# First seven rotary tiles on VectorE with their splits in turn, and sums, chunk roundings and second root moved in the passage between attention and feed-forward

## What is computed

```python
h = modulate(rms_norm(x, g_pre_mix), sh1, sc1)
qa, ka, va, qi, ki, wi, qb, kb, vb, ga, gb = project(h, pos, w_in)   # rope on qa, ka, qi, ki, qb, kb
oa, ob = mixer(qa, ka, va, qi, ki, wi, qb, kb, vb)                   # top-k attention, differential attention
m = sigmoid(ga) * (oa @ w_o_a) + sigmoid(gb) * (ob @ w_o_b)
x = x + gt1 * rms_norm(m @ w_out, g_post_mix)
h = modulate(rms_norm(x, g_pre_ffn), sh2, sc2)
f = (silu(h @ w_gate) * (h @ w_up)) @ w_down
x = x + gt2 * rms_norm(f, g_post_ffn)
```

## Time and profile before

| | us |
|---|---|
| median of 3 runs | 1034.13 |
| the profiled execution, its own time | 1035.23 |
| its span, first to last instruction | 1033.4 |
| PE busy in it | 964.7 (93%) |
| DVE, ACT, POOL busy | 443.1, 410.7, 375.5 |

### The profile page before, as it was taken

How to read it: one execution, slowest core, us unless ns; L and a number is a source line. 1 busy time by engine, 2 the same in 40 slices (tenths; PEclk the granted TensorE clock), 3 DMA queues, 4 the chain that set the end, 5 groups by cost and what they waited for, 6 DMA issues and landing times.

```text
span 1033.4 us, 17731 instructions
## 1 busy us (share of the span) xinstructions
PE 964.7 (93%) x7100; PEld 916.0 (89%) x7100; DVE 443.1 (43%) x869; ACT 410.7 (40%) x766; POOL 375.5 (36%) x181
## 2 busy tenths in 40 slices
PE   4887997999998999999999779999999999999995
PEld 1686897999998989988888679999999999999995
DVE  5786637898885233332100834333333333000005
ACT  4754334556556555443333733222222222222221
POOL 2131025556262331234554124444443343444440
PEclk9898998999999999999999889999999999999998
DMA  9821012222221113357855012222222221322212
GB/s 368 316 75 46 7 63 87 102 102 85 90 99 51 41 49 131 111 221 256 304 191 187 22 41 82 82 82 81 81 81 81 81 81 56 105 73 82 82 54 92
DMA packets 35600, 111.61 MB, mean 108 GB/s; under 512 B 4240, under 2 KB 9360, under 8 KB 35280
## 3 DMA queue, kind: packets, MB, share of 16 engines
q1 hardware_dynamic: 31152, 102.48, 29.0%
q10 hardware_dynamic: 4112, 6.93, 1.8%
q0 software_dynamic: 272, 1.31, 0.3%
HBM read 100.38 MB, written 10.32 MB: 107 GB/s over the span
## 4 chain that ended last, share of the span: by engine, by line
PE 75%; issue 9%; DVE 7%; ACT 4%; DMA 3%; POOL 2%; ACTq 0%; DVEq 0%; SPq 0%; POOLq 0%
PE pj L1831 25%; PE pj L1598 23%; PE pj L1870 12%; PE pvb L1728 3%; DMA raw<-in_w_ada 3%; PE pj L1607 2%; PE lg L1570 2%; PE tb L1712 2%; PE pj L1843 1%; DVE kz L1277 1%; PE lg L1893 1%; PE lg L1895 1%; PE lg L1894 1%; DVE ro L552 1%; DVE mb L1340 1%
## 5 line engine op out<-in xcount | busy, mean ns | idle before, releaser
L1076 POOL TENSOR_TENSOR wlo<-raw,whi 128x1024 fp32r<-128x1024 f32 x53 | 131.1, 2474 | 202.8 <-ACT whi L724 196.9
L1132 POOL TENSOR_TENSOR wlo<-raw,whi 128x1024 fp32r<-128x1024 f32 x41 | 105.2, 2567 | 183.7 <-ACT whi L1043 183.7
L1831 PE MATMUL pj<-hh,wlo 128*128 128x288 f32 (+1 forms) x640 | 137.4, 296 | 0.0
L1831 PE MATMUL pj<-hh,whi 128*128 128x288 f32 (+1 forms) x640 | 137.1, 295 | 0.0
L1831 PE MATMUL pj<-hl,whi 128*128 128x288 f32 (+1 forms) x640 | 136.9, 295 | 0.0
L1598 PE MATMUL pj<-hh,whi 128*128 128x288 f32 x544 | 124.7, 311 | 4.9 <-ACT zs L805 4.0
L1598 PE MATMUL pj<-hh,wlo 128*128 128x288 f32 x544 | 117.9, 298 | 0.0
L1598 PE MATMUL pj<-hl,whi 128*128 128x288 f32 x544 | 117.9, 299 | 0.0
L1831 PEld LDWEIGHTS pj<-hh,wlo 128*128 128x128 f32 x640 | 103.4, 189 | 0.0
L1831 PEld LDWEIGHTS pj<-hh,whi 128*128 128x128 f32 x640 | 102.9, 188 | 0.0
L1831 PEld LDWEIGHTS pj<-hl,whi 128*128 128x128 f32 x640 | 102.8, 188 | 0.0
(11 more groups left out here) (216 smaller groups left out, 2015.0 us busy)
## 6 DMA issues: line engine op xcount, KB each, us to landing
raw<-in_w_s SPq DMA_DIRECT2D x94, 512.0 KB, 3.5
rawa<-in_w_ada SPq DMA_DIRECT2D x32, 512.0 KB, 6.1
rawd<-in_w_d SPq DMA_DIRECT2D x16, 704.0 KB, 4.1
raw<-in_w_ada SPq DMA_DIRECT2D x16, 512.0 KB, 10.1
g_raw<-gz ACTq DMA_DIRECT2D x16, 288.0 KB, 2.1
gate<-g_raw SPq DMA_DIRECT2D x8, 576.0 KB, 3.9
rawv<-in_w_v SPq DMA_DIRECT2D x8, 324.0 KB, 5.0
xt<-in_xT SPq DMA_DIRECT2D x2, 1152.0 KB, 6.7
```

What stands on the lines that cost most here:

```text
L1076: pool.tensor_tensor(wlo[:, slot(c), :], raw_of(c), whi[:, slot(c), :].bitcast(F32), ALU.subtract)\
L1132: pool.tensor_tensor(wlo[:, slot(c), :], raw[:, raw_slot(c), :], whi[:, slot(c), :].bitcast(F32), ALU.subtract).then_inc(w_lo, 1)
L1831: ins = mm(pj[tile % 2][:, h, 0:HALF + 2 * h], w[:, slot(C_GU + q), b:b + P], x[h][:, kc, :], start=(kc == 0 and w is whi and x is hh2), s ...
```

## The change

`N_VEC` is 7: kb0 and qb0 are turned on DVE as well. For these seven the split stands right behind the tile's `end` (and the rounding of value chunks), and `hi` behind the split; the split of qb0 so stands ahead of the three top-k rounds. kb1 keeps POOL, and its split stays in unit 2. In the passage POOL sums the squares of tiles 0 to 5 only and `stat1` takes a third matmul for tile 6; `hi(C_GU+2)` and the second root move behind `scaled(1, 4)`, `hi(C_GU+3)` and `hi(C_GU+4)` ahead of the last root, and `ada_ends(5)` behind the first half's work on DVE. `N_SUM0` renumbers the counts of POOL's sums.

```diff
+N_VEC = ROPE_AT[("qb", 0)] + 1
 def schedule():
-    def project(c, waiting, values=()):
-
-        s.extend([("part", AT[c], 0, KC)] * (AT[c] >= N_FIRST) + [("split", w) for w in waiting] + [("end", AT[c])]
-                 + [("vsplit", k) for k in values])
-        return [AT[c]]
-
-    last = []
+    def project(c, values=()):
+
+        s.extend([("part", AT[c], 0, KC)] * (AT[c] >= N_FIRST) + [("end", AT[c])] + [("vsplit", k) for k in values])
+        if ROPE_AT[c] < N_VEC:
+            s.extend([("split", AT[c]), ("hi", AT[c])])
+
     for c, values in zip(ROPES[:N_KI], ((4, 5), (6, 7), (), (), ())):
-        last = project(c, last, values)
-    s += [("split", c) for c in last] + [("vload",)]
+        project(c, values)
+    s += [("vload",)]
...
-    last = project(("kb", 0), [])
-    last = project(("qb", 0), last)
+    project(("kb", 0))
+    project(("qb", 0))
     topk(3)
-    last = project(("kb", 1), last)
+    project(("kb", 1))
...
-    split_in[2] = last
+    split_in[2] = [AT[("kb", 1)]]
...
+        N_SUM0 = (KC - 1) + (KC - 2)
...
             act.activation(hf1[1][:, :, HALF:HALF + 2], ada[:, 3 * KC:4 * KC, :], ACT.Copy).then_inc(shift_ready, 1)
-            hi(C_OUT + KC - 1 + RING)
...
                 scaled(1, kc)
-                if kc == 1:
+                if kc == 4:
                     act.wait_ge(rstd_ready, 2)
                     act.wait_ge(stat_full, 3)
                     rms_half(0)
+                    hi(C_GU + 2)
                 if kc % 2:
                     squares_x1(1, kc // 2)
+            hi(C_GU + 3)
+            hi(C_GU + 4)
             act.wait_ge(rstd_ready, 3)
...
-                        if c < C_DN:
+                        if 0 < t and c < C_DN:
...
-                        if r >= N_KI:
+                        if r >= N_VEC:
                             turns_of(pool, c, r)
...
-                if d < KC - 1:
+                if d < KC - 2:
                     squares(0, d, acc1, sq1)
...
-                    if ROPE_AT.get(CH[s[1]], N_KI) < N_KI:
+                    if ROPE_AT.get(CH[s[1]], N_VEC) < N_VEC:
                         rope(s[1])
...
-            for n in range(3, 6):
+            for n in range(3, 5):
                 ada_ends(n)
...
             for h in range(2):
+                if h:
+                    ada_ends(5)
                 v.wait_ge(ysq_ready, KC + h)
...
             def stat1(h):
-                stat_half(h, [acc1, sq1[:, KC - 1, :]], [(acc_ready, 2 * (KC - 1)), (ysq_ready, KC + h)])
+                stat_half(h, [acc1, sq1[:, KC - 2, :], sq1[:, KC - 1, :]],
+                          [(acc_ready, N_SUM0), (ysq_ready, KC - 1), (ysq_ready, KC + h)])
```

More of the change, by code:

```diff
@@ L1109, in squares @@
                 if d:
-                    pool.wait_ge(acc_ready, (n + 1) * (KC - 1) + d)
+                    pool.wait_ge(acc_ready, (N_SUM0 if n else KC - 1) + d)
                 pool.tensor_tensor(acc[:, :], acc[:, :], sq[:, d, :], ALU.add).then_inc(acc_ready, 1)
             def y_tile(d):
-                if d < KC - 1:
+                if d < KC - 2:
                     squares(0, d, acc1, sq1)
@@ L1847, in stat3 @@
             def stat3(h):
-                for i, (x, sem_, n) in enumerate(((acc2[:, :], acc_ready, 3 * (KC - 1)),
+                for i, (x, sem_, n) in enumerate(((acc2[:, :], acc_ready, N_SUM0 + KC - 1),
                                                   (sq2[:, KC - 1, :], ysq_ready, 2 * KC + 1 + h))):
```

## The result

| | kernel before | changed kernel |
|---|---|---|
| median (lowest to highest), us | 1033.71 (1033.14 to 1037.04), 4 runs | 1017.58 (1015.15 to 1019.73), 4 runs |
| profiled execution, us | 1035.23 | 1019.73 |
| its span, us | 1033.4 | 1017.6 |

The ratio is 0.9833, 95% interval 0.9814 to 0.9852: faster by 16.1 us, where 20.0 were predicted. The time lies in the range of 1009 to 1022, 3.6 above the number given. The page of the changed kernel, first part (compare): PE has four matmuls more, the third product of `stat1`, and loses less around its work.

The account below looks back on a forecast made before the run. PE, busy 93% of the span, was taken to lose most of its time up to the feed-forward in four waits (5.37, 5.38, 5.65, 4.51 us). Terms 6.0, 4.0 and 10.0 sum to 20.0; 1034.1 less 20.0 is 1014, range 1009 to 1022.

Parts of the forecast that it names:

- The passage, 10.0: Passage into the feed-forward: reordered sums, roots and roundings remove PE's waits, gaining 10.0 us; ends 7.0 and 10.5.
- (e): Passage: hi(C_GU+3), hi(C_GU+4) run beside stat2(1); the 4.51 wait goes, following tiles at full clock end near 612.5, not 623.
- The clock rival: Head and passage: remaining waits bring 1.2 GHz back each time; head 5.0, passage 7.5, time 1017.6; chance 0.14.
- the prediction's last sign of being wrong: Behind the short waits: a granted clock near 0.66 would show the prediction wrong.
- The head, 6.0: First five rotary tiles: hi behind the split frees ro, first indexer head 6.0 us earlier; ends 3.1 and 7.1.
- clock term, +0.5: Head: +0.5 us, taken between up to 1.6 more from the indexer's clock and up to 0.8 less from the last lo.
- the tile count: Head: a tile falls from 7.05 to 6.55 us; counted through, the last rest comes 5.5 earlier.
- kb0 and qb0, 4.0: Ahead of attention unit 0: six DVE instructions of 0.75 replace six POOL ones of 1.42, gaining 4.0; ends 2.5 and 7.0.
- The race: kb0: DVE's second rest instruction, issued at 153.45, narrowly passes POOL's lo at 153.6; losing costs 1.5 us.
- The rival of the shared way: Head and kb0: POOL's shifted subtraction falls fully on the next tile's products; neither wins over 1; 1023; chance 0.10.
- PE alone setting units 0 to 4: Attention units 0 to 4: PE, not DVE, sets them, gaining 3.0 more, time 1011; chance 0.06.
- fall behind in branch B: Branch B's 20 attention units: extra POOL holds in 15 use up DVE's idle time; kernel slower, 1039; chance 0.04.

Follow-up runs that it names:

- e4: Changed kernel with the three top-k rounds moved from behind qb0 to ahead of kb0; 1016.46 us, ratio 0.9834.
- e7: Changed kernel with kb0 and qb0 turned on POOL again, splits and hi there in the earlier order; 1019.71 us, ratio 0.9857.
- e6: Changed kernel with unread dummy matmuls in two PE waits: 16 ahead of the first indexer head, 18 ahead of kc 5; 1016.00 us, ratio 0.9822.
- e5: Changed kernel with hi(C_GU+2) moved behind the second-half loop; 1014.17 us, ratio 0.9804.
- e9: Changed kernel with two edits: hi(C_GU+2) behind the second-half loop and the three top-k rounds ahead of kb0; 1014.46 us, ratio 0.9807.
- e11: Changed kernel with hi(C_GU+2) back in its old place ahead of the first scaled; 1017.25 us, ratio 0.9830.
- e2: Changed kernel with rotary tiles, splits and roundings put back as before, the passage kept as changed; 1023.79 us, ratio 0.9899.
- e3: Changed kernel with the rounding hi ahead of the split again in the seven rotary tiles; 1023.14 us, ratio 0.9909.
- e10: Changed kernel with POOL's seventh sum, stat1 of two products and the last modulation columns ahead of DVE's first inverse, as before; 1019.43 us, ratio 0.9854.
- e8: Changed kernel with hi(C_GU+3) and hi(C_GU+4) back behind the first silu; 1024.32 us, ratio 0.9899.

## Why the prediction was near, and where it was off

The mechanisms were right: `ro` at 0.76, `zc` of the later tiles longer, no wait on the sum, none on `wlo`, PE's start in the passage, the new wait at kc 5, and DVE binding units 0 to 5. The gain was short by about 4 us, in three terms; by the stretches of the two profiles they came to 4.4, 3.5 and 7.9, 15.8 instead of 20.0. Some of that lies in the execution that was profiled: the fastest, 1015.15, is within 1.2 us of the forecast. One reading at the start is too strong: the four waits, 20.9 us, are not most of what PE loses up to the feed-forward. It is idle for 57.0 of the first 610.69 us, 16.0 of it waiting for loads in the first 35; no term hangs on this.

**The passage, 10.0, measured 7.9.** Up to the second half every step came out: moved by the 7.98 that PE is earlier at `stat1`, PE's start is at 573.0 (predicted 573.0) and the end of the first half at 582.1 (582.0). The wait at kc 5 was 2.49, not 3.4. The step that failed in this profile is in (e), "the following tiles, at full clock". The 18 matmuls from kc 5 on took 4.51 (584.89 to 589.40) at the clock of 0.66; in e4, whose clock was 1.00 there, 2.52:

```profile
582.82 0.40 PE L1613 MATMUL pj<-hh,whi 128*128 128x290 f32 x1 [2.49 <-DVE hl L1222]
...
585.34 4.04 PE L1759 MATMUL lg<-sq,ones 128*128 128x288 f32 x16
```

With the 0.8 of `stat2(1)` this makes 2.8, less 0.9 for the shorter wait 1.9, and 2.1 are missing. With the same wait and the clock up, e4 and e7 have passages of 47.56 and 47.41, a gain of 10.6 and 10.7, the 10.0 and most of the 0.9 of a shorter wait. Where the wait is filled (e6) or taken away (e5, e9, e11), the clock stayed up each time.

The clock rival had put the passage at 7.5 and the whole at 1017.6, which is the measured median. That the two agree so well is luck: its head term was 5.0, not 4.4, and for another reason. Its mechanism did show, as the prediction's last sign of being wrong would have it: behind all four short waits of this profile the clock came down (0.83 over 10 us around the head, unit 0 and PE's start in the passage, 0.66 behind kc 5). What that cost depends on who sets the pace behind the wait. At the head it is 0.4 (e6). In unit 0 it is nothing, since DVE binds; at PE's start it is nothing either, since the first half ends 17.5 us behind `stat1` with the low clock as without it (e5, clock 1.00), so PE doesn't set the pace there. Behind kc 5 PE has no gap, sets the pace itself and pays in full.

**The head, 6.0, measured 4.4.** Its clock term, +0.5, came to nothing, and with the wait filled (e6) it would have been 0.4. The other 1.1 are the tile count. The evacuations of qi0 to qi3 came 1.3, 1.2, 2.0 and 2.7 earlier, where 1.0, 3.0, 3.5 and 4.0 were counted: the tile of qi0 won nothing. There POOL's subtraction began while DVE's key rest ran, lasted 3.14 (55.36 to 58.50) and held `zc` for 1.2:

```profile
57.16 1.96 DVE L545 TENSOR_TENSOR zc<-z,cos 128x576 f32<-128x576 f32 x1 [0.86 <-ACT zs L807]
...
55.36 3.14 POOL L1080 TENSOR_TENSOR wlo<-raw,whi 128x1024 fp32r<-128x1024 f32 x1 [10.22 <-ACT whi L726]
```

And `hi`, now ahead of the next evacuation, took 1.05. The 2.0 counted for this tile (3.0 less 1.0) is about all that `ro` won (2.07), so hardly any of either was charged to it. The later tiles won 0.8 each, more than the 0.5 counted, as `zc` was held for 0.37 and not 0.7.

**kb0 and qb0, 4.0, measured 3.5.** The race went as told (the second key rest got ahead of POOL, by 0.06 us: 149.01 and 149.07), but its other side was not priced: POOL then stands still, its subtraction lasts 3.27 instead of 2.6, and `zc` of qb0 comes out 0.6 later. That nothing more would come of it, since DVE binds the units behind, was right: 36.27 before, 36.33 after; e4, which frees DVE, wins 1.2 there. In the order before, the low clock had a part in these units as well: e2, whose clock was back 3 us into unit 0, comes to unit 5 after 35.32.

The rival of the shared way is out: what POOL holds on the next tile's products is 0.37 in qi1 to qi3 and 1.2 in qi0 and qb0, not the whole. PE alone setting units 0 to 4 is out by the chain, still DVE's key rest (176.65), and by e4. DVE did not fall behind in branch B (the stretch to `stat1` is 0.18 shorter).

## What to carry to other kernels

When two engines exclude each other, count every hold from both sides: which of the two is issued first, and what the one that comes second is late for. Putting the rounding behind the split in seven tiles was worth 5.6 us by the medians (e3); turning two of these tiles on the faster engine, in the new order, 2.1 by the medians and 3.3 in the trace (e7), which overlaps with the first. And a new short wait of TensorE isn't priced by its length: ask who sets the pace behind it, and where TensorE does, add what the following work would cost at the lower clock, as a cost that comes in some executions and not in others. See first whether the wait can be put where TensorE doesn't need the result yet, as e5 does with one line.

## What the runs showed that was not expected

**The same wait doesn't always bring the clock down.** Of seven profiles with 2.3 to 2.5 us of waiting at kc 5, the granted clock in the 9 us behind it was 0.66 in one (the changed kernel), 0.81 to 0.84 in three (e2, e3, e10) and 1.00 in three (e4, e7, e8); in the four without an idle PE there (e5, e6, e9, e11) it was 1.00. At the first indexer head, nine waits of 2.3 to 2.4 us brought it down nine times. The price goes with the clock: the passage takes 50.20 in the first, 48.89 and 48.71 in e2 and e3, 47.56 and 47.41 in e4 and e7. The Trainium skill (TensorE: Matmul & The Clock Gate, Part 1) says that the monitor which sets the clock runs freely and doesn't restart with a kernel, so the moment of a change varies; a mixed outcome for one wait fits that, though no run here shows the monitor itself.

**A stretch that no edit touches goes both ways.** Stretches of the changed kernel and of e5, where both have the same code:

```profile
34.00:40.00 6.00, 5.20 (x33) 4.56 (x34) 3.59 (x11) 3.47 (x7) 0.00 (x0) 0.72 0.81 246
```

```profile
34.00:40.00 6.00, 5.55 (x42) 5.55 (x43) 4.66 (x13) 4.35 (x8) 0.00 (x0) 1.00 0.97 327
```

The clock was 0.72 in eight of the 13 profiles and 1.00 in five (e3, e5, e6, e7, e10), and with the new order of the head (all but e3, e2 and the kernel before) the first indexer head stands at 82.5 to 83.1 with the one, at 80.5 to 81.4 with the other: about 2 us that no edit makes, which is why a gain like that of e4 is better read between milestones than from medians.

**DVE instructions with one tile input are held too.** In e4 a TENSOR_SCALAR of 128x512 took 1.87 instead of 0.43 beside POOL; in the changed kernel one of 128x8 at 83.49 took 1.69, where the same line takes 0.17 at 98.42:

```profile
83.49 1.69 DVE L1322 TENSOR_SCALAR wis<-vt 128x8 f32<-128x8 f32 x1 [0.67 <-ACT vt L879]
...
98.42 0.17 DVE L1322 TENSOR_SCALAR wis<-vt 128x8 f32<-128x8 f32 x1 [3.09 <-ACT vt L879]
```

POOL's subtraction runs from 82.78 to 85.15 there, and the first ends right behind it, at 85.18. The Trainium skill (SBUF — State Buffer, Who interferes with whom) counts `tensor_scalar` among the operations that can take the shared ports; the trace agrees.
